# RWKV-7 decays and factors of the batch after next made inside the state scan, with a third buffer for r and the decays

## What is computed

```python
def rwkv7_scan(r, decay, k, v, a_vec, b_vec, s0):
    def step(s, inp):
        rt, wt, kt, vt, at, bt = inp
        sa = jnp.einsum('bhij,bhj->bhi', s, at)
        s = s * wt[:, :, None, :] + sa[..., None] * bt[:, :, None, :] + vt[..., None] * kt[:, :, None, :]
        return s, jnp.einsum('bhij,bhj->bhi', s, rt)
...
    y_f, sr_f = rwkv7_scan(r, dec_f, kd_f, vc, -kk, kk * a_f, sr_f0)
    y_b, sr_b = rwkv7_scan(flip_t(r), flip_t(dec_b), flip_t(kd_b), flip_t(vc),
                           flip_t(-kk), flip_t(kk * a_b), sr_b0)
```

## Time and profile before

| | us |
|---|---|
| median of 3 runs (2226.18 to 2231.54) | 2227.45 |
| the profiled execution, its own time | 2229.23 |
| its span, first to last instruction | 2227.4 |
| its mean granted TensorE clock, share of full | 0.922 |
| TensorE busy | 1943.7 (87%) |
| VectorE busy | 1049.3 (47%) |
| ScalarE busy | 837.6 (38%) |
| GpSimd busy | 283.4 (13%) |

### The profile page before, as it was taken

The page is one execution under the profiler, slowest core; times in us unless marked ns, Lnnn a source line. Parts: engine busy times, 40 slices in busy tenths (PEclk is TensorE's granted clock), DMA queues, the critical chain, the costliest instruction groups (busy, mean ns, idle before and its releaser), DMA issues.

```text
span 2227.4 us, 32378 instructions
## 1 busy us (share of the span) xinstructions
PE 1943.7 (87%) x13395; PEld 1549.4 (70%) x13395; DVE 1049.3 (47%) x1931; ACT 837.6 (38%) x1408; POOL 283.4 (13%) x550
## 2 busy tenths in 40 slices
PE   6899998967985798999989989898687668899998
PEld 2799445633554598999979965464354547799998
DVE  0335427754565544343342544384556645543332
ACT  1533534253333535333253345324324334533321
POOL 2000000015555000000000000000553420000000
PEclk9999999978996799999999999999787669999999
DMA  7433333202130143443443423323101003344332
GB/s 256 133 116 105 101 114 123 95 25 76 58 115 20 33 152 95 127 120 108 126 126 111 125 82 114 114 86 100 57 11 48 2 1 109 104 114 133 110 118 85
DMA packets 267768, 214.06 MB, mean 96 GB/s; under 512 B 7209, under 2 KB 259400, under 8 KB 267368
## 3 DMA queue, kind: packets, MB, share of 16 engines
q1 hardware_dynamic: 264640, 204.39, 30.2%
q0 software_dynamic: 2736, 7.54, 1.1%
q10 hardware_dynamic: 248, 0.07, 0.0%
HBM read 209.10 MB, written 2.88 MB: 95 GB/s over the span
## 4 chain that ended last, share of the span: by engine, by line
PE 69%; DVE 11%; ACT 8%; POOL 7%; issue 3%; DMA 1%; DVEq 0%; ACTq 0%; POOLq 0%
PE bank L547 11%; PE bank L549 10%; PE bank L548 10%; PE bank L603 8%; PE bank L598 7%; POOL cst L1129 4%; POOL lora L1127 3%; PE bank L1046 3%; PE bank L1047 3%; PE bank L1048 3%; PE bank L609 3%; PE bank L787 2%; PE bank L499 1%; ACT h L1193 1%; PE bank L713 1%
## 5 line engine op out<-in xcount | busy, mean ns | idle before, releaser
L549 PE MATMUL bank<-scr_rounded 128*128 128x384 f32 (+1 forms) x1312 | 442.3, 337 | 0.0
L603 PE MATMUL bank<-h,ring 128*128 128x384 f32 x640 | 243.9, 529 | 21.9 <-DVEq L337 17.9
L547 PE MATMUL bank<-scr_rounded 128*128 128x384 f32 x672 | 230.5, 343 | 25.7 <-DVE scr_rounded L1606 24.2
L549 PEld LDWEIGHTS bank<-scr_rounded 128*128 128x128 f32 (+1 forms) x1312 | 248.3, 189 | 1.0
L548 PE MATMUL bank<-scr_rounded 128*128 128x384 f32 x672 | 228.1, 339 | 0.0
L1601 DVE TENSOR_TENSOR scr_rounded<-ring,scr_rounded 128x2048 fp32r<-128x2048 f32 (+1 forms) x64 | 136.0, 2126 | 177.9 <-ACT scr_rounded L1184 177.0
L547 PE MATMUL bank<-scr_rounded,gate_rounded 128*128 128x384 f32 (+1 forms) x640 | 214.8, 336 | 4.3 <-DVE scr_rounded L1601 4.3
L548 PE MATMUL bank<-scr_rounded,gate_rounded 128*128 128x384 f32 (+1 forms) x640 | 214.5, 335 | 0.0
L603 PEld LDWEIGHTS bank<-h,ring 128*128 128x128 f32 x640 | 124.7, 204 | 115.0 <-issue 48.6
L598 PE MATMUL bank<-ring,scond 128*2 128x256 f32 x768 | 181.5, 390 | 19.7 <-DVE mg L1591 6.0
L1601 DVE TENSOR_TENSOR scr_rounded<-ring,gate_rounded 128x2048 fp32r<-128x2048 f32 (+3 forms) x64 | 130.1, 2033 | 105.8 <-ACT gate_rounded L1184 105.2
(11 more groups left out here) (357 smaller groups left out, 3238.4 us busy)
## 6 DMA issues: line engine op xcount, KB each, us to landing
ring<-in_w_in_dram SPq DMA_DIRECT2D x56, 1024.0 KB, 5.3
ring<-in_w_ada_dram SPq DMA_DIRECT2D x48, 1024.0 KB, 5.3
ring<-in_w_ffn_in_dram SPq DMA_DIRECT2D x88, 512.0 KB, 5.1
ring<-in_w_ffn_out_dram SPq DMA_DIRECT2D x32, 704.0 KB, 4.6
ring<-in_w_out_dram SPq DMA_DIRECT2D x8, 1024.0 KB, 5.0
ring<-in_w_po_a_dram SPq DMA_DIRECT2D x4, 1024.0 KB, 6.4
ring<-in_w_po_b_dram SPq DMA_DIRECT2D x4, 1024.0 KB, 5.4
ring<-in_w_po_c_dram SPq DMA_DIRECT2D x4, 1024.0 KB, 6.2
```

Source lines behind the costliest of these rows:

```text
L547: pe.matmul(o, w_hi[:, k, :], right[0][k], start=k == 0, stop=False)
L549: ins = pe.matmul(o, w_lo[:, k, :], right[0][k], start=False, stop=k == nk - 1)
L603: ins = pe.matmul(b[:, 0:T], w[:, k, 128 * (j % 2):128 * (j % 2) + 128], h[:, k, :], start=k == 0, stop=k == KD - 1)
```

## The change

- `loras`, `logs`, `exps` and `terms` of batch n+1 move into pass n: `exps(2n+2)` and `logs(2n+2)` after scan step 0, `terms(2n+2)`, `loras(2n+3)` and `decays(2n+3)` after step 1, `logs(2n+3)` and `exps(2n+3)` after step 2, `terms(2n+3)` after step 3. In pass 0, which has no scan, they stand ahead of `inverses(0)` and `merges(0)`. Before, `exps(2n+2)` came after the scan on ScalarE, and `terms(2n+2)`, `logs(2n+3)`, `terms(2n+3)` after `inverses(n)` on VectorE. At the time of pass n it is batch n-1 that is in the scan, so the batch being prepared is two later than the one scanned.
- What the scan still reads (the r factor `fr`, the decays `es` and `ee`) gets three buffers in place of two. `ar` is split into `fa` (two buffers) and `fr` (three), stored contiguously; ScalarE and VectorE no longer wait for Y(n-2) before they write them.
- Room for it: the two transposed inverses `Zbn` and `ZbT` now overlap in `Zb`, so the second transpose waits for the first; `Tt` moves into `Zb`, and `kd0` into the place of `Tt`.
- Side steps: 14 ahead of `merges(0)` as before, 4 in place of 2 ahead of the other merges, and none in place of 2 after each merge.

```diff
@@ -215,16 +215,26 @@
...
-        ar = [[take(768, 6, 2, 64) for _ in range(2)] for _ in range(2)]
+        fa = [[take(T, 6, 64) for _ in range(2)] for _ in range(2)]
+        fr = [[take(T, 6, 64) for _ in range(2)] for _ in range(3)]
+        def a_and_r(n, d, rows, c):
+            i, k = n % 2, n % 3
+            start, apart = (2 * i + d) * T + 64 * c, (4 + 2 * (k - i)) * T
+            return scr[rows, start:start + 2 * apart].rearrange("p (s q) -> p s q", s=2)[:, :, 0:64]
...
-        Zbn, ZbT = take(1024, 32, 32), take(1024, 32, 32)
-        Gs, Ds, Dx, aa, kd0 = [take(T) for _ in range(5)]
+        Zb = take(1408)
+        Zbn, ZbT = (Zb[:, j:j + 1024].rearrange("p (u q) -> p u q", u=32) for j in (0, T))
+        Tt = Zb[:, 768:1152].rearrange("p (u q) -> p u q", u=12)
+        Gs, Ds, Dx, aa = [take(T) for _ in range(4)]
...
-        srow = Zbn[0:64, :, :].rearrange("p a b -> p (a b)").rearrange("p (n j) -> p n j", n=16)
+        srow = Zb[0:64, 0:1024].rearrange("p (n j) -> p n j", n=16)
...
@@ -980,14 +989,15 @@
...
                             scan_step(n - 1, s)
+                            if s == 1 and n < 3:
+                                loras(2 * n + 3)
                         outputs(n - 1)
...
                         factors(n)
-                        fill((14, 2, 2, 2)[n])
+                        if n == 0:
+                            loras(3)
+                        fill((14, 4, 4, 4)[n])
                         merges(n)
-                        if n < 3:
-                            loras(2 * n + 3)
-                        fill(2)

@@ -1384,23 +1394,19 @@
...
                     hp, d = groups[g]
-                    i = hp % 2
+                    i, k = hp % 2, hp % 3
                     act.wait_ge(S["rw_logs"], told("rw_logs", l, g + 1))
                     G6, D6, Dx6 = (t.rearrange("p (c q) -> p c q", c=6) for t in (Gs, Ds, Dx))
-                    if g >= 4:
-                        if d == 0:
-                            side_work("Y", l, hp - 2)
-                        act.wait_ge(psum_ready, filled("Y", l, hp - 2))
-                    A(es[i][d][:, d, :], G6[:, :, 31], ACT.Exp, scale=-C0).then_inc(*step())
-                    A(es[i][d][:, 1 - d, :], D6[:, :, 63], ACT.Exp, scale=-C0).then_inc(*step())
-                    A(ar[i][d][:, :, 0, :], (Dx6, D6)[d], ACT.Exp, scale=(-C0, C0)[d]).then_inc(*step())
-                    A(ar[i][d][:, :, 1, :], (D6, Dx6)[d], ACT.Exp, scale=(-C0, C0)[d]).then_inc(*step())
+                    A(es[k][d][:, d, :], G6[:, :, 31], ACT.Exp, scale=-C0).then_inc(*step())
+                    A(es[k][d][:, 1 - d, :], D6[:, :, 63], ACT.Exp, scale=-C0).then_inc(*step())
+                    A(fa[i][d], (Dx6, D6)[d], ACT.Exp, scale=(-C0, C0)[d]).then_inc(*step())
+                    A(fr[k][d], (D6, Dx6)[d], ACT.Exp, scale=(-C0, C0)[d]).then_inc(*step())
                     act.wait_ge(*last())
...

-                    i = n % 2
+                    i = n % 3
                     for d in range(2):
@@ -1483,18 +1489,23 @@
...
                             scan_step(n - 1, s)
-                    if n < 3:
-                        exps(2 * n + 2)
+                            if n < 3 and s == 0:
+                                exps(2 * n + 2)
+                            if n < 3 and s == 1:
+                                decays(2 * n + 3)
+                            if n < 3 and s == 2:
+                                exps(2 * n + 3)
                     if n < 4:
                         if n:
-                            if n == 3:
-                                side_work("Y", l, n - 1)
+                            side_work("Y", l, n - 1)
                             act.wait_ge(psum_ready, filled("Y", l, n - 1))
+                        else:
+                            exps(2)
                         factors(n)
+                        if n == 0:
+                            decays(3)
+                            exps(3)
                         merges(n)
-                        if n < 3:
-                            decays(2 * n + 3)
-                            exps(2 * n + 3)
                 for hp in range(4):
@@ -1869,22 +1880,21 @@
...
                     i = hp % 2
-                    at, bt, es1, es0 = ar[i][d], BT[i][d], es[i][d][:, 1, :], es[i][d][:, 0, :]
+                    k = hp % 3
+                    bt, es1, es0 = BT[i][d], es[k][d][:, 1, :], es[k][d][:, 0, :]
                     side_work("al", l, g)
...
                     ts(kdd, aa, P(l, "k_a", hp), oka[:, hp:hp + 1], mult, add).then_inc(*step())
-                    if g >= 4:
-                        dve.wait_ge(psum_ready, filled("Y", l, hp - 2))
                     stt(out=bt[:, :, 0, :], in0=c6(kkb[hp]), scalar=-1.0, in1=c6(aa), op0=mult, op1=mult).then_inc(*step())
...
                     tt(bt[:, :, 0, :], bt[:, :, 0, :], c6(Gs), mult).then_inc(*step())
-                    tt(at[:, :, 0, :], at[:, :, 0, :], c6(kkb[hp]), mult).then_inc(*step())
-                    tt(at[:, :, 1, :], at[:, :, 1, :], c6(pc[:, r_ + hp, :]), mult).then_inc(*step())
+                    tt(fa[i][d], fa[i][d], c6(kkb[hp]), mult).then_inc(*step())
+                    tt(fr[k][d], fr[k][d], c6(pc[:, r_ + hp, :]), mult).then_inc(*step())
                     here, after = (slice(0, 5), slice(1, 6)) if d == 0 else (slice(1, 6), slice(0, 5))
-                    tt(ee[i][d][:, here], es1[:, here], es0[:, after], mult).then_inc(*step())
+                    tt(ee[k][d][:, here], es1[:, here], es0[:, after], mult).then_inc(*step())
                     dve.wait_ge(*last())
@@ -1914,6 +1924,7 @@
...
                     dve.transpose(Zbn.rearrange("p u j -> p j u"), W).then_inc(*step())
+                    dve.wait_ge(*last())
                     dve.transpose(ZbT.rearrange("p u i -> p i u"), W.rearrange("p j i -> p i j")).then_inc(*step())
@@ -2012,19 +2023,25 @@
...
                             scan_step(n - 1, s)
-                            if s == 0 and n < 3:
+                            if n < 3 and s == 0:
                                 logs(2 * n + 2)
+                            if n < 3 and s == 1:
+                                terms(2 * n + 2)
+                            if n < 3 and s == 2:
+                                logs(2 * n + 3)
+                            if n < 3 and s == 3:
+                                terms(2 * n + 3)
                         side_work("Y", l, n - 1)
...
                         factors(n)
+                        if n == 0:
+                            terms(2)
+                            logs(3)
+                            terms(3)
                         inverses(n)
-                        if n < 3:
-                            terms(2 * n + 2)
-                            logs(2 * n + 3)
-                            terms(2 * n + 3)

```

More of the change, by code:

```diff
@@ L132, in step_kernel @@
         lora = sb("lora", [128, 4, 512])
-        small = sb("small", [128, 96])
+        small = sb("small", [128, 112])
         banks = [ctx.enter_context(nc.psum_tensor(f"bank{i}", [128, 512], fp32)) for i in range(8)]
@@ L237, in step_kernel @@
         hse = reuse[:, 2304:2560].rearrange("p (d x q) -> p d x q", d=2, x=2)
-        Tt = reuse[:, 2560:2944].rearrange("p (u q) -> p u q", u=12)
+        kd0 = reuse[:, 2560:2944]
         term = lora[:, 0, 0:256]
-        es = [[small[:, 24 * i + 12 * d:24 * i + 12 * d + 12].rearrange("p (s c) -> p s c", s=2) for d in range(2)] for i in range(2)]
-        ee = [[small[:, 48 + 12 * i + 6 * d:54 + 12 * i + 6 * d] for d in range(2)] for i in range(2)]
+        es = [[small[:, 24 * i + 12 * d:24 * i + 12 * d + 12].rearrange("p (s c) -> p s c", s=2) for d in range(2)] for i in range(3)]
+        ee = [[small[:, 72 + 12 * i + 6 * d:78 + 12 * i + 6 * d] for d in range(2)] for i in range(3)]
         tot = small[:, 16:28].rearrange("p (a c) -> p a c", a=4)
@@ L833, in grams @@
                             for r in hr:
-                                at, bt = ar[i][d][r, c, 0, :], BT[i][d][r, c, 0, :]
+                                at, bt = fa[i][d][r, c, :], BT[i][d][r, c, 0, :]
                                 ins = pe.matmul(b[r, 64 * c:64 * c + 64], (bt, at)[d], (at, bt)[d], start=True, stop=True)
@@ L870, in factors @@
                                         ins = pe.matmul(pair[h][hr[k], cols], BT[i][d][hr[h], c, k ^ h, :],
-                                                        ar[i][d][hr[h], c, :, :].rearrange("p s q -> p (s q)"), start=True, stop=True)
+                                                        a_and_r(n, d, hr[h], c), start=True, stop=True)
                             ins.then_inc(psum_ready, 2)
@@ L953, in outputs @@
                                 if scanned(d, 0)[0] != c:
-                                    ins = pe.matmul(b[hr[h], 64 * c:64 * c + 64], HS[hr[h], d, c, :], ar[i][d][hr[h], c, 1, :], start=False, stop=True,
```

(5 more changed lines are left out.)

## The result

| | before | after |
|---|---|---|
| median, us (lowest to highest, 5 runs each) | 2227.45 (2225.17 to 2231.72) | 2240.75 (2238.95 to 2245.43) |
| ratio, with its 95% interval | | 1.0058 (1.0042 to 1.0074) |
| span of the profiled execution, us | 2227.4 | 2237.2 |
| mean granted clock | | 0.927 |

The kernel became slower by 13 us, or 0.6%; the forecast was 24 us faster. The starts of the inversions answer to the earlier trace rows; this is the timeline of GpSimd in the kernel after.

A forecast was written before the change was run, and what follows sets the result against it. The prediction took GpSimd's inversions, the RWKV phase's longest chain, and the waits between them as the bound. Savings of 63.8 us less costs of 39.6 gave 24.2 us, a forecast median of 2203, range 2185 to 2219.

The forecast's parts named there:

- B and C: Intervals between inversion starts, B batch 1 to 2, C 2 to 3; added 7 us each, 11 for layer 1's C.
- signs of being wrong: Wrong if part 2 stays above 12 us, part 1 of B stays 48, or batches 0/1 scan clock falls under 0.8.
- part 2: From the first matmul of the merges to the next inversion; forecast 8.0 us, saving 63.8 in all.
- part 1: From inversion start to the first matmul of the merges; moved work there forecast to cost 39.6 us in all.
- A: Interval from the inversion start of batch 0 to batch 1's; forecast cost 3.8 us from VectorE and GpSimd slowing each other.
- rival 3: Each moved instruction holds GpSimd off for its whole length: 9.4 us instead of 3.8 in A; time 2214, chance 0.12.
- (i) and (ii): Scan steps 0 to 1, ScalarE waits for logs: 1.5 us; steps 1 to 2, terms ahead of R's copy: 4.5.
- (iii): Scan step 2 to the copy of Y: second logs, exps and terms lengthen 7.6 us to 9.9, added 2.
- (iv): VectorE evicts a GLA side step ahead of taking out the inverse, and waits for TensorE: added 1 us.
- 2: Lower-clock rival: new waits bring B and C to 1.2 GHz, some 17 us each; loss 12, time 2239, chance 0.08.
- 1: Full-cover rival: moved work falls into VectorE's gaps, B and C add nothing beyond GpSimd; time 2175, chance 0.10.
- 4: Rival: costs and savings cancel (B and C at 14), or next batch's first gram still comes late; 2227, chance 0.08.

The follow-up runs named there:

- e1: The changed kernel with ScalarE emptying the side banks ahead of its three new waits for logs and terms; 2215.1 us, ratio 0.9938 to the kernel before.
- e4: The kernel before with the side steps regrouped alone, four ahead of the merges and none behind; 2244.6 us, ratio 1.0073.
- e10: e9 with side_work behind VectorE's take-out of the inverse and one side step instead of four ahead of merges of batches 1 and 2; 2211.0 us, ratio 0.9922.
- e9: e1 with the second terms of each batch put back behind VectorE's take-out of the inverse; 2210.5 us, ratio 0.9921 to the kernel before.

## Why the prediction was wrong, point by point

**What failed.** The sentences "The side steps (1.6 us each) are its cover" and "The three buffers, `kd0`, the regrouping ... cost nothing that I can find". Cover that has a wait of its own is none. A side step holds one of two side banks until ScalarE or VectorE empties it; the change put ScalarE's new waits for `logs` and `terms` ahead of that emptying. I named what is queued behind the waits on ScalarE (scaled states, the copy of U) and left out the item that TensorE's side steps wait for. Measured, by e1: 20.0 us in B and C of layer 0 and 4.4 in layer 1, on a forecast of 0. It turns the gain of 11 us that e1 has into a loss of 13. And the regrouping is not free: alone it cost the kernel before 18.6 us (e4). The prediction's signs of being wrong did not catch this: part 2 stayed below 12 us, part 1 of B did not stay at 48, and over the scans of batches 0 and 1 in layer 0 (553 to 600 and 622.75 to 673.5 us) the granted clock was 0.85 and 0.90, not under 0.8.

**Part 2.** Forecast 8.0 (9.0 in layer 0's A), saved 63.8. Measured 7.4 to 10.1, saved 60.4. Right.

**A.** Forecast 3.8 each, measured 4.7 and 4.5. Right in size: the inversion grew by 4.3 us, not by rival 3's 9.4. For each of the 17 moved instructions with two SBUF inputs the inversion grew by 0.25 us, and they themselves grew too, most from 0.55 to over 0.8. The Trainium skill (SBUF — State Buffer, "SBUF: two separate sides") gives the shared port to whichever of the two engines starts first, for its whole instruction, while the other waits. The trace agrees in that both engines pay; that GpSimd alone pays the whole length, as the prediction read the rule, it does not bear out.

**B and C.** Forecast 7 for both B and layer 0's C, 11 for layer 1's C. Measured 18.1 and 9.2 for B in layers 0 and 1, 21.7 and 11.8 for C; with the rows first 7.5, 6.7, 12.3 and 9.9. By VectorE's timeline (first copies of R in steps 1 and 2, copy of Y, take-out), e1 against before:

| us added | forecast | layer 0 B | layer 0 C | layer 1 B |
|---|---|---|---|---|
| start to the R of step 1 | -2 | -2.9 | +0.8 | -2.5 |
| to the R of step 2, (i) and (ii) | +6 | +6.0 | +6.4 | +4.4 |
| to Y, (iii) | +2 | +2.4 | +2.2 | +3.5 |
| to the merges, (iv) | +1 | +1.9 | +2.9 | +1.3 |

The sizes hold within 2 us once the rows are out of the way, but for layer 0's C: its scan had begun at once in the kernel before (first R 2.0 us after the start), so nothing was there to be saved, and (iv) is 2.9. In (iv) there, e1's VectorE waits for the matmuls that turn a row (L509), and its TensorE for a gate that ScalarE takes out behind a table load:

```profile
668.55 0.16 DVE L1600 TENSOR_TENSOR mod<-bank,par 128x4 f32<-128x4 f32 x1 [2.46 <-PE bank L509]
...
670.82 2.82 PE L613 MATMUL bank<-h,ring 128*128 128x384 f32 x8 [2.30 <-ACT arena L1186]
```

**The rivals.** 2, the lower clock, gives nearly the measured time (2239). Its condition, B and C over 14 us each, held in layer 0 and not in layer 1 (9.2 and 11.8), and the clock did not come near 0.75 in layer 0. These are the windows of part 1 of layer 0's B and C, columns as in the earlier trace rows: two before, two after, two of e1.

```profile
552.60:601.00 48.40, 43.19 (x487) 25.39 (x485) 26.03 (x73) 15.46 (x39) 31.55 (x61) 0.98 0.20 67
619.90:665.20 45.30, 40.80 (x496) 23.84 (x495) 25.08 (x71) 15.05 (x39) 31.34 (x61) 1.00 0.46 141
...
547.20:613.80 66.60, 49.01 (x504) 28.10 (x502) 38.53 (x93) 20.96 (x47) 32.36 (x61) 0.90 0.20 64
622.75:689.80 67.05, 50.92 (x510) 27.80 (x510) 39.26 (x93) 20.69 (x48) 33.91 (x61) 0.90 0.31 95
...
551.35:607.30 55.95, 48.62 (x502) 28.46 (x499) 39.57 (x93) 20.50 (x47) 34.06 (x61) 0.94 0.23 76
616.20:673.80 57.60, 47.88 (x510) 27.02 (x508) 40.08 (x93) 20.38 (x47) 35.67 (x61) 0.97 0.36 111
```

The granted clock fell from 0.98 and 1.00 to 0.90. TensorE stood still for 17.6 and 16.1 us after, for 5.2 and 4.5 before. Of the 20.0 us that e1 gives back here, 16.7 are standing still and 3.4 are busy time, nearly all of it in C. So the stalls are the larger part, and matmuls at the lower clock are a smaller part of the same loss. Eight of L608 took 3.57 us behind the stall of 6.28 us, at a granted clock of 0.50, and 1.89 at 1.00 earlier in the same scan:

```profile
565.05:568.50 3.45, 3.45 (x8) 0.83 (x8) 0.00 (x0) 0.00 (x0) 3.12 (x5) 0.50 0.00 0
555.50:557.30 1.80, 1.80 (x10) 0.58 (x9) 1.66 (x7) 0.00 (x0) 1.57 (x4) 1.00 0.72 274
```

1 and 3 fell with A and B as measured. 4, that nothing comes of it, put B and C at 14, and they were at 15.2 on the mean, but it gave no place for it.

**Left open.** Not shown is how the 14.2 us of e4 in layer 0 divide between the row's wait (2.81 us shown), the side steps now in part 1, and the next scan's later start (first R of C at 5.1 us instead of 2.0).

## What to carry to other kernels

When an in-order engine gets a new wait, list everything behind it that some other engine needs *in order to go on at all*, banks to be emptied above all, and not only what the main chain wants: emptying first was worth 25 us here. Filler work is cover only as long as its own outputs are taken away, and its price is that of the place where it stands: two steps that are free beside `terms` cost some 3 us once `terms` is gone. And leave in place what the remaining wait can hold: the version with the lowest median has the second `terms` where it was.

## What the runs showed of the hardware

A VectorE instruction on two 128x384 tiles took 0.55 us with GpSimd idle and mostly 0.8 to 1.05 beside it, more than the 0.2 added that I had assumed; the last one of a `terms` (L1903) often stayed at 0.56. GpSimd's inversion grew by about a quarter of a microsecond for each such instruction in A. And the granted clock made a shorter part 1 not always a gain: that of layer 1's B was 2.1 us shorter in e10 than in e9, and the same work behind it (157 matmul records) ran at 0.67 instead of 0.81 of full clock. Part 2 in e10, then in e9:

```profile
1676.10:1686.40 10.30, 10.28 (x157) 7.06 (x158) 8.76 (x16) 4.13 (x9) 0.00 (x0) 0.67 0.40 125
...
1677.00:1685.90 8.90, 8.84 (x157) 5.79 (x158) 7.79 (x15) 5.72 (x12) 0.00 (x0) 0.81 0.19 59
```
